# Pacing the modulation loads of a two-block transformer kernel by its projection slots, and lengthening two rings of weight slots

## The reference, cut to what matters

```python
mod = c_act @ w_ada[l] + b_ada[l]                # 1024 x 6144 per layer
sh1, sc1, g1, sh2, sc2, g2 = split(mod, 6)
h = rms_norm(x, norm1_g) * (1 + sc1) + sh1
x = x + g1 * mixer(h)                            # layers 0, 1: attention + conv + gating
h2 = rms_norm(x, norm2_g) * (1 + sc2) + sh2      # layer 2: gated linear attention, layer 3: RG-LRU
x = x + g2 * ffn(h2)
```

## Time and profile before

| | |
|---|---|
| median of 3 runs | 2781.35 us |
| the profiled execution | 2791.36 us (its span 2789.6 us) |
| PE busy | 2356.4 us, 84% of the span |
| DVE, ACT, POOL busy | 44%, 24%, 24% |
| TensorE clock, mean granted | 0.928 of 2.4 GHz |
| DMA | 934.35 MB, mean 335 GB/s over the span |
| gathered rows | 512 DMAs of 1 MB, issued between 207.6 us and about 1726 us |

### The profile page before, as it was taken

How to read it: one execution, slowest core, us unless ns; L and a number is a source line. 1 busy time by engine, 2 the same in 40 slices (tenths; PEclk the granted TensorE clock), 3 DMA queues, 4 the chain that set the end, 5 groups by cost and what they waited for, 6 DMA issues and landing times.

```text
span 2789.6 us, 25669 instructions
## 1 busy us (share of the span) xinstructions
PE 2356.4 (84%) x9276; PEld 1240.1 (44%) x9276; DVE 1232.2 (44%) x2873; ACT 662.4 (24%) x1860; POOL 657.1 (24%) x831
## 2 busy tenths in 40 slices
PE   7899877778788989977877787987998989789988
PEld 3676433333333577433333333446443456644433
DVE  1336666776664325667667755553200022330001
ACT  1213232333233122333223333111111123111111
POOL 1103333333332102433433332101222000122200
PEclk9999999998889989999999989987999999899999
DMA  9749999999997647999999997863799235669980
GB/s 366 305 151 365 422 421 421 421 421 421 421 422 315 273 196 316 386 421 421 421 422 421 421 421 329 329 263 136 324 421 421 115 121 213 254 280 421 421 339 16
DMA packets 130127, 934.35 MB, mean 335 GB/s; under 512 B 14289, under 2 KB 16337, under 8 KB 16593
## 3 DMA queue, kind: packets, MB, share of 16 engines
q0 software_dynamic: 114768, 835.96, 72.5%
q1 hardware_dynamic: 15232, 96.75, 9.0%
HBM read 1070.02 MB, written 1.05 MB: 384 GB/s over the span
## 4 chain that ended last, share of the span: by engine, by line
PE 47%; DMA 31%; DVE 16%; ACT 4%; issue 2%; SPq 0%; DVEq 0%; POOL 0%; ACTq 0%; POOLq 0%
PE units L738 12%; PE units L1222 12%; PE accs L992 11%; DMA arena<-rows,idx 11%; DMA wide<-rows,idx 8%; DMA wide<-experts 5%; DMA ring<-stream 4%; DVE wide L1974 3%; DVE arena L1974 2%; PE units L753 2%; DMA arena<-experts 2%; PE units L1187 2%; PE accs L1270 2%; ACT arena L1461 1%; PE accs L821 1%
## 5 line engine op out<-in xcount | busy, mean ns | idle before, releaser
L992 PE MATMUL accs<-wide,arena 128*128 128x512 f32 x1040 | 515.8, 651 | 147.0 <-ACT arena L1461 146.8
L992 PE MATMUL accs<-arena 128*128 128x512 f32 x1008 | 481.4, 632 | 96.5 <-ACT arena L1461 96.3
L992 PEld LDWEIGHTS accs<-wide,arena 128*128 128x128 f32 x1040 | 211.2, 208 | 437.7 <-issue 250.4
L1222 PE MATMUL units<-wide,arena 128*64 128x512 f32 (+1 forms) x1728 | 372.4, 601 | 26.2 <-DMA wide<-experts 21.2
L647 POOL DMA_INDIRECT wide<-rows,idx x260 | 245.7, 945 | 607.7 <-PE accs L992 419.6
L992 PEld LDWEIGHTS accs<-arena 128*128 128x128 f32 x1008 | 201.9, 203 | 371.1 <-issue 247.4
L647 POOL DMA_INDIRECT arena<-rows,idx x252 | 238.3, 946 | 361.7 <-PE accs L992 325.4
L738 PE MATMUL units<-arena,ring 128*128 128x256 f32 (+1 forms) x1344 | 300.4, 386 | 27.3 <-ACT arena L1351 14.0
L1324 ACT ACTIVATE arena<-units 128x512 f32<-128x512 f32 (+1 forms) x186 | 106.5, 575 | 841.5 <-PE units L738 300.8
L738 PEld LDWEIGHTS units<-arena,ring 128*128 128x128 f32 x1344 | 256.8, 200 | 72.4 <-issue 36.6
L1222 PE MATMUL units<-arena 128*64 128x512 f32 (+1 forms) x960 | 235.4, 594 | 17.1 <-DMA arena<-experts 10.9
(11 more groups left out here) (317 smaller groups left out, 2158.3 us busy)
## 6 DMA issues: line engine op xcount, KB each, us to landing
wide<-experts POOLq DMA_DIRECT2D x123, 1024.0 KB, 18.4
wide<-experts SPq DMA_DIRECT2D x93, 1024.0 KB
wide<-ada POOLq DMA_DIRECT2D x88, 1024.0 KB, 10.2
arena<-experts POOLq DMA_DIRECT2D x69, 1024.0 KB, 20.3
ring<-stream SPq DMA_DIRECT2D x62, 1024.0 KB, 6.5
arena<-experts SPq DMA_DIRECT2D x51, 1024.0 KB
arena<-side SPq DMA_DIRECT2D x8, 1024.0 KB, 8.3
wide<-ada SPq DMA_DIRECT2D x7, 1024.0 KB, 13.4
```

Of the source, the lines that this page charges most:

```text
L992: ins = mm(o[:, half * 512:(half + 1) * 512], diag[:, i % (2 * GROUP), :], row_slot(PICKS * l + i)[:, D + half * 512:D + (half + 1) * 512] ...
L1222: ins = mm(o[j * n:(j + 1) * n, :], act[:, j * n:(j + 1) * n], exp_slot(l, i)[:, c * 512:(c + 1) * 512], start=start, stop=stop, skip_grou ...
```

## The change

Five edits are made together.

1. `ada_loads` for the first ring-full of a layer takes a slot number. Ahead of its loads 0 and 1 POOL now waits for stream slot `slot + 1` of the mixer to have landed, ahead of loads 2 and 3 for `slot + 2`, of 4 and 5 for `slot + 3`, of load 6 for `slot + 4`, where `slot` is the first stream slot of the mixer. Before layer 0 the wait for the eighth modulation slot of SP is dropped. The other loads wait as before.
2. The modulation ring has 7 places; `ada_sums` moves to a new tile `spare` of one slot.
3. The expert slots have 13 places: seven in `wide`, the tile of the PEER keys `keys_sb` (idle in the last two layers), four in `arena`, and `spare`.
4. The four loads of one step of an extra tile increment one semaphore, of which there are four in turn, and PE waits once for a step in place of four times.
5. The tile of zeros shrinks from 512 to 128 columns; the banks of `accs` are opened by 16 matmuls of 128 columns and not by 4 of 512.

```diff
-ADA_RING = 6
+ADA_RING = 7
...
-EXP_AT = SLOT_AT[0:7] + SLOT_AT[10:14]
+EXP_AT = SLOT_AT[0:7] + (("keys", 0),) + SLOT_AT[10:14] + (("spare", 0),)
 NE = len(EXP_AT)
...
+def extra_step(l, i):
+    return ((l - DEPTH) * EXTRA + i - OWN) // 4
...
+        spare = sb("spare", [P, SLOT])
...
-        zeros = sb("zeros", [P, 512], BF16)
+        zeros = sb("zeros", [P, P], BF16)
...
-        ada_sums = wide[:, ADA_RING * SLOT:(ADA_RING + 1) * SLOT]
+        ada_sums = spare[:, :]
...
-                                :, bass.ds(e, 1), s, :], cond=used).then_inc(extra_landed[exp_at(l, i)], 16)
+                                :, bass.ds(e, 1), s, :], cond=used).then_inc(
+                                    extra_landed[extra_step(l, i) % 4], 16)
...
-            def ada_loads(first, end):
+            def ada_loads(first, end, slot=None):
                 for i in range(first, end):
+                    if slot is not None:
+                        wait_slot(pool, slot + 1 + (i - first) // 2)
                     pool.wait_ge(ada_free(i), ada_uses(i) - 1)
                     pool.dma_start(ada_piece(i), ada[i]).then_inc(
                         ada_landed[(i - ADA_FIRST) % ADA_RING], 16)
...
-            pool.wait_ge(first_landed[ADA_FIRST - 1], 16)
-            ada_loads(ADA_FIRST, ADA_FIRST + ADA_RING)
+            ada_loads(ADA_FIRST, ADA_FIRST + ADA_RING, 0)
             pool.dma_start(arena[:, 0:FIRST_CONST], first_const[0]).then_inc(const_landed, 16)
...
                 if l:
-                    ada_loads(before_of(l), before_of(l) + ADA_RING)
+                    ada_loads(before_of(l), before_of(l) + ADA_RING,
+                              SLOT_OF["q" if l < DEPTH else "gq" if l == DEPTH else "lru_g", l])
...
-                    for i in loads:
-                        sems = exp_landed if i < OWN else extra_landed
-                        pe.wait_ge(sems[exp_at(l, i)], 16 * landings_to(l, i, i >= OWN))
+                    if loads[0] >= OWN:
+                        n = extra_step(l, loads[0])
+                        pe.wait_ge(extra_landed[n % 4], 16 * 4 * (n // 4 + 1))
+                    else:
+                        for i in loads:
+                            pe.wait_ge(exp_landed[exp_at(l, i)], 16 * landings_to(l, i))
...
-                for b in range(4):
-                    mm(acc[b][:, :], zeros[:, 0:P], zeros[:, :], start=True, stop=False, skip_group_check=True)
+                for b in range(16):
+                    mm(accs[:, b * P:(b + 1) * P], zeros[:, :], zeros[:, :], start=True, stop=False,
+                       skip_group_check=True)
```

More of the change, by code:

```diff
@@ L309, in uses_before, with landings_to @@
     return m // NE
-def landings_to(l, i, extra):
+def landings_to(l, i):
     at = ((l - DEPTH) * LOADS + i) % NE
-    return sum(1 for n in range((l - DEPTH) * LOADS + i + 1) if n % NE == at and (n % LOADS >= OWN) == extra)
+    return sum(1 for n in range((l - DEPTH) * LOADS + i + 1) if n % NE == at and n % LOADS < OWN)
+def extra_step(l, i):
+    return ((l - DEPTH) * EXTRA + i - OWN) // 4
 def program(nc, x, w, side, experts, ada, small, first_const, gla_const, keys, rows, out):
@@ L385, in program @@
         exp_landed = [sem(f"exp_landed{i}") for i in range(NE)]
-        extra_landed = [sem(f"extra_landed{i}") for i in range(NE)]
+        extra_landed = [sem(f"extra_landed{i}") for i in range(4)]
         exp_read = [sem(f"exp_read{i}") for i in range(NE)]
@@ L528, in exp_slot @@
         def exp_slot(l, i):
-            where, at = EXP_AT[((l - DEPTH) * LOADS + i) % NE]
-            return (wide if where == "wide" else arena)[:, at:at + SLOT]
+            where, at = EXP_AT[exp_at(l, i)]
+            if where == "keys":
+                return keys_sb[:, :, :].rearrange("p a b -> p (a b)")[:, at:at + SLOT]
+            return {"wide": wide, "arena": arena, "spare": spare}[where][:, at:at + SLOT]
         def exp_at(l, i):
```

## The result

The change makes the kernel slower. The kernel after has a median of 2797.01 us (2792.13 to 2807.42, 12 runs), the kernel before, run beside it, 2779.43 us (12 runs): a ratio of 1.0068 with a 95% interval of 1.0055 to 1.0082, about +19 us. The forecast was "no change", 2781.5 us, with a range up to 2795. The result lies just outside it, at rival 3's 2797. The profiled execution after took 2802.2 us (span 2800.5).

A forecast was written before the change was run, and what follows sets the result against it. The prediction took PE's stream and expert matmuls, and the first two layers' row gathers, as the bound. Its terms, -10.0 + 0.5 - 2.7 - 1.0 + 9.4 + 3.0 + 1.0 = +0.2 us, gave 2781.5 us, range 2766 to 2795.

The forecast's parts named there:

- rival 3: Mixers: pieces held back until slots land, over 9 us per slot beside a pair; +15.4, about 2797 us; chance 0.11.
- The experts: Expert stretches of both layers: two loads fewer after the first freed place, -5.0 us each, -10.0 together.
- The stall ahead of `gv` 0: Third mixer: PE idle about 11 us because DVE adds late piece 7 before returning the z banks; start +8.2 us.
- The small edits: Zeros and step waits: narrower zero matmuls +0.5 us per layer, +1.0 together; one wait in place of four, 0.
- the forecast's own signs of being wrong: Gv 0 idle under 4 us, expert waits falling much less than 5 us a layer, or first mixer keeping three waits.
- all three waits go: First mixer: its stream-slot waits and slow slot vanish, -6.9 us; with later costs, net -2.7.
- Third mixer: Layer 2's mixer: late pieces delay gv 0 by 8.2 us, its slot runs 1.7 slower; net +9.4, bounds +6 and +13.
- Fourth mixer: Layer 3's mixer: pairs of modulation loads make two stream slots late by 0.9 to 2.4 us; +3, bounds 0 and +6.
- Output projections: Layer 2: one more expert load competes with the stream slots, +0.5 us; layer 3: 0.
- Rival 2: Mixers: two queues share equally, a contended slot takes 7.1 us; -6.0, about 2775 us; chance 0.20.
- Rival 1: Third mixer: the stall does not come or is hidden; -20.5, about 2761 us; chance 0.11.
- Rival 4: First mixers: pacing has no effect, waits come from something other than POOL's loads; +2 to +4, 2785 us; chance 0.06.

The follow-up runs named there:

- d1: Kernel with the longer rings and no pacing, given pacing in layer 3 only, one load per landed slot instead of two: 2782.62 us, one run.
- a1: Changed kernel with the pacing undone everywhere and all other edits kept: 2775.95 us, ratio 0.9995 to the kernel before.
- f1: Kernel before, with only the expert loads beside the output projections held until the fourth stream slot landed: 2762.34 us, ratio 0.9944.
- a4: Changed kernel with the pacing kept in layers 0 and 1 alone: 2778.91 us, ratio 0.9999 to the kernel before.

## Why the prediction was wrong

**What held.** The experts: -5.0 each forecast, -4.8 and -5.4 measured. The stall ahead of `gv` 0 with every link of its chain, the burst of five behind the masks (at 85 us for 80), and the landing of slot 2 at 48 us with nothing beside it (POOL's row of 48.12 is released by it). The small edits: the zeros take 1.05 us a layer for 1.02, so +0.03 and not +0.5. One of the forecast's own signs of being wrong was met: the first mixer did not lose its three waits, it has four.

**The step that failed** is in the first mixer: "a pair of modulation slots takes 5.0 us and is nearly done when the next stream slot's data begin". It is not, for the reason shown by the chains of after and of `d1`: the pair's issue is tied to the landing that PE has waited for, so it goes out 0.6 to 1.8 us ahead of the next stream slot (2.5 for the first), and that slot takes 8.2 to 9.3 us beside it. The premise that all three waits go (-6.9) fell; 5.8 us of waits took the place of 5.2. The two first mixers, forecast at -3.7 together, came to about +3.5.

**Third mixer, mis-sized**: +9.4 forecast (bounds +6 and +13), +14.5 measured. `gv` 0 began 7.5 us later, counted from the norm, where +8.2 was forecast, and its slot ran 2.4 us longer (forecast 1.7). The missing 5 us lie behind: the seven loads that POOL issues at 1773.87 us make `gv` 1 late by 2.43 us and slow by 1.6, and `gg` 1, which was to wait 0.5 us less, waits 3.01 for 2.77. I had counted what the wait delays on DVE, but not that all that POOL has behind the waiting load is let go at once.

**Fourth mixer, mis-sized**: +3 forecast, +7.0 measured: 2.13 + 2.97 us on two slots, and 2.2 us by which the eight slots ran slower (the one behind the longer wait at a granted clock of 0.83). The seventh place was put at nothing because PE would only wait longer for DVE's product. It did, 2.70 us for 0.77, and the mixer is no longer by it; but what was left out is that PE comes out of that wait at half its clock, 1.65 us in the output projection.

**Output projections, mis-sized**: +0.5 in layer 2 and nothing in layer 3, measured +0.8 and +3.0 with the pacing; without it about +3 in layer 2 (+5.0 in `a1`) and +1.6 in layer 3, the columns. The forecast looked at the place where the two more loads are issued for one layer alone, and the four stream slots were late there before the change as well, which `f1` shows to be worth more than any one of its terms.

**The rivals.** Rival 3 (slower, 2797 us, chance 0.11) is nearest, but that its total agrees to the microsecond is partly luck. Its deciding point, over 9 us for each slot beside a pair, was met by three of five (9.10, 9.19 and 9.28 us; 8.19 and 8.44 in the others). Its split was not as told: `gv` 0 landed no later than the forecast had it, and the stretch behind `gv` 0, the first mixer and the output projections carried what it had put on that landing. It also said of the 9.4 to 9.7 us that they "were measured beside six waiting loads, not two"; by the landings they were three and five (see `d1`). Rival 2, equal halves, would have every contended slot at 7.1 us. About that number does appear, but only beside a single waiting load (`d1`), where two loads have to land in any case; beside two, 8.2 to 9.3 us speak against it. So the rule of the Trainium skill, "DMA: Bandwidth & Descriptors", section "Queues, rings and completion order", that the engines take turns between queues a packet at a time, does not by itself give the shares seen here. Rival 1 fell with the stall. Rival 4 comes near in the first two mixers, where the pacing gained nothing, but not for its reason: their late slots lie beside POOL's loads, and the one slot with nothing beside it, of 43.00 us, landed in 4.8 us.

Open: what makes one execution's first mixers 5 us longer than another's of the same program, and why PE's clock fell ahead of the columns in most kernels with the longer rings but not in `a4`.

## What to carry to other kernels

A load that is released by the landing of another is not spaced out by this: once the stream is late, one landing releases both and they collide each time, and the loads that stand behind the waiting one come as a burst. Look instead for the one short stretch where a stream with two places meets a deep queue of loads that nobody needs yet, and hold these until the last slot of that stream has landed; here that cost the experts nothing and gave 16 us. And a shorter stretch by more buffers is a gain only if the earlier issue does not fall on another stream: count its loads where they are issued, not only where they are waited for.

## What the runs showed of the hardware

How long a stream slot issued by SP takes, against 1 MB loads of POOL's queue that are out when it is issued, grows with the first two of them and hardly beyond. It took 4.6 us alone, 6.61 to 7.59 beside one (`d1`), 8.2 to 9.3 beside a pair that went out 0.6 to 1.8 us ahead of it, 9.05 beside six (88.82 us in the trace of after) and 9.65 beside twelve. I had expected either half whatever waits, or a share that falls on with six.

A wait that costs nothing on PE's path can still be paid for behind it: after 2.70 us of idleness the granted clock was 0.50, and 16 matmuls of four columns took 3.43 us to the next slot where they took 1.78 at 1.00. It did not happen each time: in `a4` PE waited 2.34 us at the same place and the columns ran at 1.00.
